# Another order for the 64 slots of an expert in the MoE layer of a hybrid encoder on Trainium2

## The reference, cut to what matters

```python
def hierarchical_moe(h, w_grp, b_grp, w_exp, b_exp, w_gate, w_up, w_down):
    ...
    top_v, top_i = lax.top_k(in_grp, TOP_K_IN_GROUP)          # 2 of 32 experts for each token
    top_w = jax.nn.softmax(top_v, axis=-1) * grp_w
    expert_id = g_sel[:, None] * EXPERTS_PER_GROUP + top_i
    combine = jnp.sum(jax.nn.one_hot(expert_id, N_EXPERTS, dtype=f32) * top_w[..., None], axis=1)
    y = jnp.zeros_like(x)
    for e in range(N_EXPERTS):
        hid = jax.nn.silu(x @ w_gate[e]) * (x @ w_up[e])
        y = y + combine[:, e:e + 1] * (hid @ w_down[e])
    return y.reshape(B, T, D)
```

## Time and profile before

| what | value |
|---|---|
| median of 3 runs | 790.31 us (789.97 to 791.11) |
| the profiled execution's own time | 789.99 us |
| its span | 788.2 us |
| granted clock of TensorE, mean | 0.983 |
| PE busy | 735.7 us, 93% |
| DVE, ACT, POOL busy | 226.4, 146.5, 85.5 us |
| moved by DMA | 234.76 MB |
| the 32 scatters of POOL | 2560 packets, 4.20 MB |

### The profile page before, as it was taken

How to read it: one execution, slowest core, us unless ns; L and a number is a source line. 1 busy time by engine, 2 the same in 40 slices (tenths; PEclk the granted TensorE clock), 3 DMA queues, 4 the chain that set the end, 5 groups by cost and what they waited for, 6 DMA issues and landing times.

```text
span 788.2 us, 13656 instructions
## 1 busy us (share of the span) xinstructions
PE 735.7 (93%) x6148; PEld 371.3 (47%) x6148; DVE 226.4 (29%) x455; ACT 146.5 (19%) x319; POOL 85.5 (11%) x81
## 2 busy tenths in 40 slices
PE   5999999999999999999999999999999899988950
PEld 3444454464455466555454455545445355433510
DVE  3008782005566257211111111111111111111126
ACT  5252330024255443000000000000000000000004
POOL 0542340000000121000000000000000000000002
PEclk9999999999999999999999999999999999999995
DMA  9430230401450548999999999999999999999964
GB/s 325 120 106 20 87 108 1 160 4 59 184 243 2 229 197 352 377 422 428 424 422 428 423 426 421 425 425 423 425 426 423 424 421 421 420 420 420 410 264 198
DMA packets 36828, 234.76 MB, mean 298 GB/s; under 512 B 5778, under 2 KB 7186, under 8 KB 18976
## 3 DMA queue, kind: packets, MB, share of 16 engines
q1 hardware_dynamic: 34208, 229.66, 71.5%
q0 software_dynamic: 2560, 4.20, 1.4%
HBM read 227.55 MB, written 10.49 MB: 302 GB/s over the span
## 4 chain that ended last, share of the span: by engine, by line
PE 74%; DMA 19%; SPq 2%; ACT 2%; DVE 1%; issue 1%; DVEq 0%; POOLq 0%
PE bank L487 21%; PE bank L792 18%; DMA arena<-in_w_up 17%; PE bank L815 10%; PE bank L772 8%; PE bank L655 4%; PE bank L699 3%; SPq L419 2%; PE bank L616 1%; PE bank L688 1%; PE bank L673 1%; PE bank L794 1%; PE bank L795 1%; PE bank L804 1%; DMA arena<-in_x 1%; PE bank L718 1%
## 5 line engine op out<-in xcount | busy, mean ns | idle before, releaser
L792 PE MATMUL bank<-arena 128*64 128x512 f32 x928 | 207.0, 597 | 11.4 <-DMA arena<-in_w_up 10.6
L487 PE MATMUL bank<-arena 128*128 128x512 f32 x384 | 167.0, 594 | 0.0
L792 PEld LDWEIGHTS bank<-arena 128*64 128x64 f32 x928 | 68.5, 138 | 144.9 <-issue 135.1
L815 PE MATMUL bank<-arena 128*64 128x512 f32 x512 | 116.9, 598 | 0.5 <-ACT arena L1100 0.5
L487 PEld LDWEIGHTS bank<-arena 128*128 128x128 f32 x384 | 72.3, 190 | 89.8 <-issue 88.6
L772 PEld LDWEIGHTS bank<-arena 128*128 128x128 bf16 x3072 | 96.2, 98 | 23.9 <-issue 23.4
L772 PE MATMUL bank<-arena 128*128 128x64 bf16 x3072 | 100.6, 193 | 0.0
L1095 ACT ACTIVATE arena<-bank,arena 128x256 f32<-128x256 f32 x32 | 15.2, 474 | 359.8 <-PE bank L792 316.4
L1602 POOL DMA_INDIRECT y_tok<-arena x32 | 31.2, 976 | 432.4 <-DVE arena L1473 404.4
L1466 DVE SCALAR_TENSOR_TENSOR arena<-bank,arena 128x256 f32<-128x256 f32 x32 | 15.5, 483 | 214.2 <-ACT arena L1095 214.2
L815 PEld LDWEIGHTS bank<-arena 128*64 128x64 f32 x512 | 33.9, 136 | 57.1 <-issue 54.5
(11 more groups left out here) (161 smaller groups left out, 466.8 us busy)
## 6 DMA issues: line engine op xcount, KB each, us to landing
arena<-in_w_down SPq DMA_DIRECT2D x31, 2048.0 KB, 30.8
arena<-in_w_gate SPq DMA_DIRECT2D x25, 2048.0 KB, 25.0
arena<-in_w_up SPq DMA_DIRECT2D x24, 2048.0 KB, 23.8
arena<-in_w_up SPq DMA_DIRECT2D x14, 1024.0 KB, 28.2
arena<-in_w_in SPq DMA_DIRECT2D x6, 2048.0 KB, 8.0
arena<-in_w_gate SPq DMA_DIRECT2D x12, 1024.0 KB, 27.2
arena<-y_tok SPq DMA_DIRECT2D x8, 512.0 KB, 5.5
arena<-in_x SPq DMA_DIRECT2D x4, 512.0 KB, 6.3
```

The source lines that it names most:

```text
L487: m = pe.matmul(pbank[unit_bank(n)][:], lhs(k), rhs(k), start=(k == 0), stop=(k == KC - 1))
L792: mm = pe.matmul(both, xT[:, k], gate_and_up(e, k, cols), start=(k == 0), stop=(k == KC - 1))
L815: mm = pe.matmul(pbank[5 + e % RING][64 * half:64 * half + 64, :], hidT[:, kc % 2, kc // 2], down_unit(e)[:, kc, half * 512:(half + 1) * 512],
```

## The change

The constant row `iota1` is filled with another permutation of 1 to 64. Before, slot s took rank s+1. Now slot 8a+b takes the row of rank 8b+a (from 0; the constant is one more). No instruction is added, removed or moved: on each engine the sequence is the same as before, and the source lines stand one line lower from line 50 on, two behind the constant. The value of a token's row does not depend on its slot.

```diff
 SLOTS = 64
+SLOT_RUN = 8
 RING = 3
...
     c[:, 320:384] = np.arange(SLOTS)
-    c[:, 384:448] = np.arange(1, SLOTS + 1)
+    slot = np.arange(SLOTS)
+    c[:, 384:448] = slot % SLOT_RUN * (SLOTS // SLOT_RUN) + slot // SLOT_RUN + 1
```

## The result

The changed kernel takes 798.55 us (median of 4 runs, 797.84 to 800.66), the kernel before 790.14 us beside it: ratio 1.0107, 95% interval 1.009 to 1.0123, so 8.4 us slower. The prediction was 796.8 us with a range from 793.2 to 799.2. The profiled execution took 797.84 us, 7.85 us more than the one before.

The account below looks back on a forecast made before the run. The weight stream, paced by its latest DMA engine, was taken to bound the experts' stage. Scatter packets add 7.5 us, reduced to 6.5 for overtaking, the last scatter 0: 796.8 us against the median, range 793.2 to 799.2.

Parts of the forecast that it names:

- rival 4: More than the sum, up to 799: PE's clock drops again behind 739 us (1.7 us), or the full 9.7 us; chance 0.15.
- The stream of weights paces the stage, and its latest engine paces the stream: Experts' stage, 300 to 750 us: DMA engines always busy, loads land with the latest of 16, slack 0.7 us.
- The deal to engines: Scatters: rows go to engines in short runs, not eights; the change gives eight engines 4 packets each, eight none.
- The sum: 31 scatters in the weight stream: 1.56 more packets each on a loaded engine, 0.156 us apiece, 7.5 us, lowered to 6.5.
- the step from 7.5 to 6.5: End of the weight stream: the latest engine may be relieved, the next loaded one being about 1 us ahead.
- The last scatter, 0: Scatter behind the stream: its fullest engine has 4 data packets before and after, so 0 of its 2.74 us.
- 3.7 us for the engine with the surplus: Lower bound in the scatters: the engine taking slots 32 to 35 goes from 2.8 to 3.56 packets.
- 9.7 us: Upper bound over 31 scatters: an engine with 2 packets before and 4 after.
- rival 1: Scatters: engines take eight slots in a row, so the kernel gets about 8 us faster, 782; chance 0.05.
- Rival 2: No change, 790.3: packets go to free engines, or later engines than the loaded ones set the pace; chance 0.07.
- Rival 3: Small loss, 793 to 794: surplus engine is latest (3.7 us), or PE's lead hides lag before 540 us; chance 0.18.
- What was to be seen: Changed profile: PE waits about 19 us, rate down 1 to 2%, share near half over twice 8 us, early small packets.

Follow-up runs that it names:

- the pairs of ranks: Against the kernel before: ranks dealt in pairs to the eight runs of four slots of each half in turn; 790.33 us, ratio 1.0002.
- the odd order: Changed order with slot s replaced by s xor 4, so the odd runs of four are full; 797.78 us, ratio 1.0086 against the kernel before.

## Why the prediction was right, point by point

The mechanism and the sign are shown. The size is near the upper end: 8.4 us more, where the forecast was 6.5 give or take 1.5 and the range ended 0.65 us above the measured 798.55. It lies just inside what rival 4 covered ("more than the sum, up to 799"), though not for the clock that this rival names.

- **The stream of weights paces the stage, and its latest engine paces the stream.** Right. The last landing moved by 7.5 us and the start of the last down group by 7.4 us. PE's work is the same.
- **The deal to engines.** Right, and it was the point on which the sign hung. Reading from the earlier trace rows that every engine begins with data excluded eights; the pairs of ranks excluded runs of two and single slots, which the prediction had to leave open because they gave the same sum.
- **The sum.** 1.56 packets x 31 x 0.156 us = 7.5 us, the same as the 7.5 us by which the last landing moved. That it fits to a tenth is luck. By the row counts a loaded engine has 17.3 to 17.9 us now, and the third, fifth and seventh had 10.3, 9.4 and 7.5 before: 7.5, 8.2 or 9.8 us more, and which of them was late isn't shown. The counts also give 3.65 packets for a mean loaded engine instead of the estimated 3.56, and 47 rows for the fullest expert; the scatter of 46 in the earlier trace rows was not the fullest. The term that was mis-sized is the step from 7.5 to 6.5 ("it is overtaken by one that was somewhat ahead"): it measured about 0. It took the lateness of the engines for evenly spread. Without data they stand in two groups of eight, and by the landings of the change and of the odd order four of the loaded eight are in the late group each time: the latest loaded one was about as late as the latest of all.
- **The last scatter, 0.** It took 0.7 us more in this execution (2.74 to 3.47 us). Its fullest engine has no more data than before, so the working gives no reason; in the odd order it took 5.47 us, so it varies with more than the row counts. The whole tail from the start of the last down group grew by only 0.4 us (29.7 to 30.1), so part of it was won back behind it. 7.4 plus 0.4 are the 7.8 us between the two spans. The 8.4 us of the medians hold 0.6 us that no single profile shows; the profiled execution of the changed kernel is the fastest of its four.
- **Bounds.** 3.7 us for the engine with the surplus was no bound that mattered, for that engine was early; 9.7 us was not reached. (In rival 1 the sum has 1.8 packets less, where 4 less 2.1 is 1.9; nothing hangs on it.)
- **Rival 1** (eights, 782 us) fell with the first packets of the last scatter, and with the result. **Rival 2** (no change) fell too: the late engines are not all relieved, in neither of the two loaded halves. **Rival 3** fell with the size of the loss: if PE's lead before 540 us had swallowed half, or the engine with the surplus had been the late one, it would have been under 4 us. **Rival 4**: the clock did fall, at 302 and 636 us (PEclk 0.91 in 620 to 640 us), but not behind the last wait for weights, where it would have cost time; between the two PE had a lead or waited for weights anyway.
- **What was to be seen.** PE's waits grew to 17.3 instead of 19 us, since PE was busy 2.8 us longer. The mean rate of 300 to 750 us fell from 420 to 416 GB/s, 1%. The small packets were there. The share did fall to near one half, but over some 11 us and not over twice 8: that was wrong. I took it that light engines could run ahead as far as they liked. In the load that landed at 735.1 us they were 14 to 22 us ahead of the latest one. But what SP has issued is all they have, so at the end they had stood still before (0.74 at 741 us, 0.93 at 748 us). It changes nothing in the end if the loaded engines never pause, which no view shows engine by engine.

## What to carry to other kernels

Where the DMA engines are busy all the time, count the work of each engine, not the mean: a transfer of 2% of the bytes (3.95 of 189 MB here) whose rows fall on half of the engines costs about what the late ones among these engines get more, and a load that spreads evenly is then as late as they are. For a scatter with empty rows, the partitions that are full decide it: fill short runs all over the partitions, and check on a transfer that meets idle engines whether small packets are among the first. Before tuning the order, find out which engines are late for other reasons; the free room is on the others.

## What the runs showed of the hardware

- An indirect scatter of POOL deals its 128 partitions to the engines in runs of four, and even runs share engines among themselves, as odd ones do (the pairs: 1.0002; the change: 1.0107; the odd order: 1.0086). Two neighbouring rows of 2 KB make one packet (64 of the 80 packets of a scatter). A packet of skipped rows is sent, but costs next to nothing: with hardly anything else in the scatters, their 2480 packets took 0.3% of 16 x 450 us, 9 ns each.
- The engines of one core are several microseconds apart at the end of a stream of 450 us with hardly any data in the scatters (share 0.61 and 0.51 from 746 to 750 us): eight land 5.7 us before the other eight on average. It is not by chance which ones: an order of slots that spares six of eight gained 0.3%.
- If the first run is paired with the ninth and so on, the engines at the edges of the deal, the first and the last of eight, have room for some 5 us more than the fullest had before (1.0006).
